# Second attention of a two-block transformer kernel: each pair's weight unit in one piece, second transpose behind the next scores, five other operations moved forward

## The reference, cut to what matters

```python
def _latent_token_mixer(h, kv_ctx, w_in, ...):
    k_a_c, v_a_c, k_b_c, v_b_c = kv_ctx
    proj = h @ w_in + b_in
    ...
    o_a = _windowed_attention(q_a, k_a, v_a, k_a_c, v_a_c, sink)
    o_b = _global_attention(q_b, concat([k_b, k_b_c]), concat([v_b, v_b_c]))
    return _merge_branches(o_a, o_b, proj[..., OFF_GA:], w_branch_a, w_branch_b, w_out)
```

## Time and profile before

| | before |
|---|---|
| median of three runs | 934.7 us (934.2 to 935.8) |
| the profiled execution | 935.65 us |
| its span, first to last instruction | 934.0 us |
| PE busy | 909.8 us, 97% |
| PE weight loads busy | 734.0 us, 79% |
| DVE busy | 720.4 us, 77% |
| ACT busy | 534.3 us, 57% |
| POOL busy | 161.6 us, 17% |
| mean granted TensorE clock | 0.995 |

### The profile page before, as it was taken

The page is one execution under the profiler, slowest core; times in us unless marked ns, Lnnn a source line. Parts: engine busy times, 40 slices in busy tenths (PEclk is TensorE's granted clock), DMA queues, the critical chain, the costliest instruction groups (busy, mean ns, idle before and its releaser), DMA issues.

```text
span 934.0 us, 13750 instructions
## 1 busy us (share of the span) xinstructions
PE 909.8 (97%) x4672; PEld 734.0 (79%) x4672; DVE 720.4 (77%) x1030; ACT 534.3 (57%) x830; POOL 161.6 (17%) x247
## 2 busy tenths in 40 slices
PE   8999999999999989999999999999999999999996
PEld 7888887777877878888888887666678788888885
DVE  4779476878778778887588788875668889999976
ACT  6775654475765556555433344756674676666643
POOL 7001000216600000110021001460000024444400
PEclk9999999999999999999999999999999999999998
DMA  9747744876552446887498856332235565555572
GB/s 317 201 149 221 252 139 140 265 267 195 171 179 84 135 152 220 266 271 256 162 351 295 274 167 202 97 89 88 87 112 175 168 193 174 174 174 176 171 261 72
DMA packets 100534, 176.16 MB, mean 189 GB/s; under 512 B 8560, under 2 KB 36592, under 8 KB 100352
## 3 DMA queue, kind: packets, MB, share of 16 engines
q1 hardware_dynamic: 93120, 149.87, 49.7%
q0 software_dynamic: 7184, 25.50, 8.1%
q10 hardware_dynamic: 176, 0.08, 0.0%
HBM read 174.38 MB, written 1.05 MB: 188 GB/s over the span
## 4 chain that ended last, share of the span: by engine, by line
PE 59%; DVE 4%; ACT 2%; issue 1%; DVEq 0%
PE acc L775 51%; PE turned L1245 2%; PE scores L1234 1%; PE turned L868 1%; PE turned L1347 1%; DVE wlo L1922 1%; PE turned L1134 1%; PE turned L1157 1%; PE turned L811 1%; ACT prob L1774 0%; DVE soft L2623 0%; DVE turn L2009 0%; ACT whi L1387 0%; PE turned L1249 0%; ACT turn L1831 0%
## 5 line engine op out<-in xcount | busy, mean ns | idle before, releaser
L1922 DVE TENSOR_TENSOR wlo<-raw,whi 128x1024 fp32r<-128x1024 f32 (+3 forms) x269 | 345.1, 1302 | 85.3 <-ACT whi L1387 74.6
L1387 ACT CAST whi<-raw 128x1024 fp32r<-128x1024 f32 (+3 forms) x269 | 273.4, 1034 | 163.7 <-PE acc L775 119.6
L775 PE MATMUL acc<-whi,lta_hi 128*128 128x512 f32 (+2 forms) x576 | 163.4, 399 | 0.2 <-DVEq L2498 0.2
L775 PE MATMUL acc<-whi,lta_lo 128*128 128x512 f32 (+2 forms) x576 | 155.8, 385 | 0.0
L775 PE MATMUL acc<-wlo,lta_hi 128*128 128x512 f32 (+2 forms) x576 | 155.3, 385 | 0.0
L775 PEld LDWEIGHTS acc<-whi,lta_hi 128*128 128x128 f32 x576 | 101.1, 188 | 31.8 <-issue 11.8
L775 PEld LDWEIGHTS acc<-whi,lta_lo 128*128 128x128 f32 x576 | 106.9, 188 | 22.4
L775 PEld LDWEIGHTS acc<-wlo,lta_hi 128*128 128x128 f32 x576 | 106.9, 188 | 21.9
L657 POOL DMA_DIRECT2D wm<-in_w_mod x48 | 34.5, 720 | 436.8 <-DVEq L2053 251.2
L775 PE MATMUL acc<-whi,ltb_hi 128*128 128x512 f32 (+1 forms) x268 | 73.8, 394 | 3.3 <-ACT whi L1387 2.4
L775 PE MATMUL acc<-whi,ltb_lo 128*128 128x512 f32 (+1 forms) x268 | 72.3, 388 | 0.2 <-DVE ltb_lo L2758 0.2
(11 more groups left out here) (370 smaller groups left out, 1307.1 us busy)
## 6 DMA issues: line engine op xcount, KB each, us to landing
raw<-in_w_in SPq DMA_DIRECT2D x88, 512.0 KB, 3.9
wm<-in_w_mod POOLq DMA_DIRECT2D x48, 512.0 KB, 5.5
raw<-in_w_up SPq DMA_DIRECT2D x88, 256.0 KB, 3.0
raw<-in_w_up SPq DMA_DIRECT2D x32, 512.0 KB, 4.5
raw<-in_w_down SPq DMA_DIRECT2D x32, 512.0 KB, 5.1
raw<-in_w_down SPq DMA_DIRECT2D x44, 256.0 KB, 3.2
raw<-in_w_o SPq DMA_DIRECT2D x8, 512.0 KB, 4.6
raw<-in_w_out SPq DMA_DIRECT2D x8, 512.0 KB, 3.8
```

The costliest lines, as they stand in the source:

```text
L775: ins = pe.matmul(acc[s][:, t, 0:n], lhs[part][:, kt0 + kk, tok], w[:, u % RING, kk, 0:n], start=(opens and k == 0 and kk == 0 and j == 0) ...
L1387: act.copy(whi[:, s, :, 0:n], raw[:, s, :, 0:n]).then_inc(hi_ready, 1)
L1922: dve.tensor_tensor(wlo[:, s, :, 0:n], raw[:, s, :, 0:n], whi[:, s, :, 0:n].bitcast(F32), ALU.subtract)\
```

## The change

In `attend_pairs` the second `PT` tile of a pair is transposed behind the scores of the next pair; this holds for MLA and AB. In AB the whole unit runs ahead of the values, and `ab_rest` keeps only the transposition. Four of the 24 first transposes go. ACT does one small activation on the identity ahead of its first wait for data. The copy of V0 moves behind those of `mqT` and `mkT`. `gate_on("G21")` moves ahead of a split. Around CX, ACT casts units between the groups of `hc` and goes through units ahead of the squares; DVE makes two groups of `hc` before each addition to x, and splits a unit between.

```diff
                 for p in range(n):
-                    for e in range(2):
-                        ... (wait, four transposes of prob[:, e], signal)
+                    turned_out(p, 0)
                     if p + 1 < n:
                         score(p + 1)
+                    turned_out(p, 1)
                     fill_units(p + 1)
                     ...
-            for _ in range(24):
+            for _ in range(20):
                 pe.transpose(sc[0][:, 0:P], ident[:], ident[:])
...
             def ab_rest(p):
                 if p > 0:
                     ab_turn(p - 1, 0)
-                ab_fill(p, (1,))
-            attend_pairs("AB", AB_PAIRS, ab_scores, 4, ab_values, lambda p: ab_fill(p, (0,)), ...)
+            attend_pairs("AB", AB_PAIRS, ab_scores, 4, ab_values, lambda p: ab_fill(p, range(T)), ...)
...ACT
+            act.wait_ge(ev("ident_ready"), 1)
+            act.activation(stat[:, 0, 8:9], ident[:, 0:1], ACT.Copy, scale=ident[:, 1:2])
             act.wait_ge(ev("columns_landed"), 16)
...
-            evac("V0", gv[:, :, 0:COLS])
+            ahead(last_unit("V0") + 1)
             for name, dst in (("mqT", mqT), ("mkT", mkT)):
                 t_out(name, dst.rearrange("p a b -> p (a b)"))
+            evac("V0", gv[:, :, 0:COLS])
...
-            lt_act("hc", ltb)
+            lt_act("hc", ltb, (0, 1))
+            ahead(PLAN.unit["WOB1"])
+            lt_act("hc", ltb, (2,))
+            ahead(PLAN.unit["WOB1"] + 1)
+            lt_act("hc", ltb, (3,))
+            ahead(PLAN.unit["CX"])
             act.activation(stat[:, 0, 8:9], one_col[:], ACT.Sqrt)
...
                 if c == 0:
-                    ahead(PLAN.unit["CX"])
+                    ahead(PLAN.unit["CX"] + 1)
...DVE
-            ahead(PLAN.unit["UKV0"] + 1)
             gate_on("G21", o_mem)
...
-            lt_dve("hc", ltb, modx[:, 8:16], modx[:, 0:8], sent=ctxT)
             for c in range(2):
+                lt_dve("hc", ltb, modx[:, 8:16], modx[:, 0:8], (2 * c, 2 * c + 1), sent=ctxT)
                 ... (addition to x)
+                if c == 0:
+                    ahead(PLAN.unit["WOB1"])
             ahead(PLAN.unit["CX"])
```

More of the change, by code:

```diff
@@ L860, in attend_pairs, with turned_out @@
                     fill_rest(0)
-                for p in range(n):
-                    for e in range(2):
[L863 to L869, removed]
+                def turned_out(p, e):
+                    i = 2 * p + e
+                    b, k = S_USE[f"{name}.{i}"]
+                    pe.wait_ge(s_free[b], k + 2)
+                    bank, full = t_begin(f"{name}.PT{i}")
+                    for j in range(blocks):
+                        ins = pe.transpose(bank[:, P * j:P * j + P], prob[:, e, P * j:P * j + P], ident[:])
+                    ins.then_inc(full, 1)
+                for p in range(n):
+                    turned_out(p, 0)
                     if p + 1 < n:
                         score(p + 1)
+                    turned_out(p, 1)
                     fill_units(p + 1)
@@ L1291, in ab_rest @@
                     ab_turn(p - 1, 0)
-                ab_fill(p, (1,))
-            attend_pairs("AB", AB_PAIRS, ab_scores, 4, ab_values, lambda p: ab_fill(p, (0,)), after=lambda p: ab_turn(p, 1),
+            attend_pairs("AB", AB_PAIRS, ab_scores, 4, ab_values, lambda p: ab_fill(p, range(T)), after=lambda p: ab_turn(p, 1),
                          fill_rest=ab_rest)
```

## The result

The kernel after takes 940.07 us (median of 5 runs, 939.91 to 940.60) against 934.7 us (5 runs, 934.1 to 935.8) of the kernel before: ratio 1.0058, 95% interval 1.0043 to 1.0072, so 0.6% slower. The forecast was 938.6 us, slower. Its profiled execution has a span of 938.5 us; before it was 934.0.

A forecast was written before the change was run, and what follows sets the result against it. PE, busy 909.8 of 934.0 us, was taken as the bound. 935.65 - 0.8 - 1.3 - 1.25 - 2.0 + 6.6 = 936.9 us, plus one clock fall of 1.7, gave 938.6; range 931 to 942.5.

The forecast's parts named there:

- The main step: AB: without the half unit behind the values PE waits for ACT and DVE, +1.2 us at each of seven places.
- R1: Rival: in AB the transposition is no obstacle, cover is not lost; total 927.1, or 932 with half lost; chance 0.13.
- R2: Rival: only AB's five transpositions cost, chains of pairs 0 and 2 fit, no clock fall; 934.1 us; chance 0.22.
- The chain behind pair 0: AB: DVE's norm sums and ACT's two table changes lose the half unit as cover, about +1.2 us.
- a switch: AB: one more change of matmul kind between scores and second tile, 0 to 0.1 us, taken as 0.05 a pair.
- The chain behind pair 2: AB: DVE's copy of IN3, ahead of pair 4's last exponential, loses the half unit as cover, about +1.2 us.
- The work saved: AB: a whole unit takes 2.85 us against 3.10 for two halves; less a switch, -0.2 us a pair.
- one fall of 1.7: Clock drops to half speed once behind new PE waits at the scaled x or in AB, +1.7 us.
- R3: Rival: the clock falls at most new waits, four falls of 1.7 us in AB and at CX; 943.7; chance 0.15.
- The small edits: Start, mqT and mkT, G21, MLA and CX: 0, -0.8, -1.3, -1.25 and -2.0 us.
- the new wait at the scaled x: CX: PE's 2.4 us wait goes, but PE stands 1.9 us at the transposes of the scaled x instead.
- The start: First matmul sooner by ACT's early table load, but transfers set the pace: 0, at best -0.3 us.

The follow-up runs named there:

- e1: Kernel after with AB's unit split again, first half behind the scores' second tile, second half behind the values: 930.02 us.
- e4: Kernel after with ACT's copy of a tile transposed behind the values moved behind the next pair's exponentials, PE's order unchanged: 931.10 us.
- e9: Kernel after with AB's unit in halves only behind the five pairs with a transposition (4, 5, 6, 9, 10): 932.02 us.
- e3: Kernel before with only the second transposed tile moved behind the next scores, in MLA and AB, AB's unit still in halves: 934.54 us.
- e7: e1 with the start as before: no early activation on ACT, 24 transposes: 929.83 us.
- e5: e1 with ACT's copy of a turned tile moved behind the next pair's exponentials: 927.15 us.
- e6: e5 with the unit whole ahead of the values behind pairs 7, 8 and 11 to 15, halves elsewhere: 927.32 us.
- e8: e1 with the CX edit undone on ACT and DVE: hc in one piece, table load and squares ahead of the cast of CX's first unit: 932.42 us.
- e2: Kernel before with only AB's unit in one piece between scores and values, both turned tiles still ahead of the scores: 951.31 us.
- e11: e5 with DVE's inverse of the norm sums behind the maxima of pair 2 instead of ahead of them: 927.52 us.

## Why the prediction was right

**The main step held.** That the loss sits where the half unit covered ACT and DVE was right in mechanism, in place (seven places) and in size: 1.25 a transposition against 1.2 forecast, 1.37 a chain against 1.2. e1 takes the whole loss back, e4 takes back most of it with PE's order untouched, e9 parts the transpositions from the chains. R1 (927 to 932) and R2 (934) are excluded by these. The signs came as well: with the clock up, periods of 8.78, 8.43 and 8.39 where 8.7 was forecast, the first `PT` at 2.19 behind pair 4's transposition and 2.01 behind the later ones. PE's waits there read 1.54 and 0.29, or 1.36 alone, where I said 1.8 and 0.4: the profile counts them from the end of the transposition (0.66 us long), and I had given it 0.4. The undisturbed pairs take 6.23 to 6.25 and not 6.1 to 6.2.

**The chain behind pair 0 was right in part by luck.** I gave it 1.2 for the lost half unit, and its period (from pair 2) rose by 1.37. But e1 and e3 keep the half unit, and there it is 8.02, already 0.79 above the 7.23 before. So the late tile made 0.79 of it and the whole unit only 8.60 - 8.02 = 0.58. In my sum the late tile was a switch and no more. ACT copies both transposed tiles ahead of its two table loads, and now the second comes later. PE's rows of e3, then ACT's of e3, then ACT's of the kernel before:

```profile
588.45 1.13 PE L1237 MATMUL scores<-kT_a,qT_a 64*128 64x512 f32 x4
...
595.20 0.66 PE L867 MATMUL turned<-ident,prob 128*128 128x128 f32 x4 [0.79 <-ACT prob L1777]
596.47 1.13 PE L1237 MATMUL scores<-kT_a,qT_a 64*128 64x512 f32 x4 [0.61 <-ACT prob L1777]
```

```profile
590.20 0.60 ACT L1447 ACTIVATE probT<-turned 128x512 f32<-128x512 f32 x1 [0.99 <-PE turned L867]
590.82 1.28 ACT L1441 ACT_TABLE_LOAD   x1
```

```profile
592.20 1.28 ACT L1438 ACT_TABLE_LOAD   x1
```

The first load starts 590.82 - 588.45 = 2.37 us behind the scores of pair 2 in e3, and 592.20 - 591.36 = 0.84 in the kernel before. That this delay is all of the 0.79 is read from these rows; no experiment moves it alone. The chain behind pair 2 is as forecast: its period (from pair 4) is 6.42 in e1 and 7.74 in the kernel after.

**The work saved was too high.** I took 0.25 for the unit and -0.05 for a switch, 0.2 a pair. Measured are 0.12, and the parts were wrong as well: e3 shows the late tile at -0.04, so the merged unit gives 0.1, and the whole unit took 2.94 in its place and not the 2.85 of the earlier trace rows, taken from a stretch with other neighbours. The other nine pairs gave 0.5 in all and not 1.8: 1.3 in eight periods, 0.44 of it from the late tile in the first, less the 0.8 behind the last scores. Together with the size of the places AB cost 8.4 us without falls, against 6.6.

**The clock.** I took one fall of 1.7; two came in the profiled execution, 1.6 and 1.5 us. Both followed waits in the pairs with transpositions, as forecast for "six or seven places"; the like waits at the other places were followed by none. R3 with four is too many for the profile and for the runs, which lie within 0.7 us of each other.

**The small edits** were forecast at -5.35. At ck -0.6 (-0.8), at UKV1 -1.5 (-1.3), in MLA -1.4 (-1.25) held. At CX the new wait at the scaled x came where forecast, but at 1.44 us and not 1.9, in PE's timeline of the kernel after:

```profile
340.43 1.09 PE L811 MATMUL turned<-ident,work 128*128 128x128 f32 x8 [1.44 <-DVE work L2543]
```

So like for like the edit gives 1.0 and not 0.3, and no fall came there. The start was forecast at 0, and e7 confirms it, though the profile alone seemed to say -0.96. The profiled execution comes to 935.65 - 0.96 - 0.6 - 1.5 - 1.4 - 2.6 + 8.4 + 3.1 = 940.1: gains of 1.7 more than forecast, 1.0 of it chance, stand against losses of 3.2 more. That the total came within 1.5 us owes something to these two misses having opposite signs.

**The rule that I set against the trace.** In TensorE: Matmul & The Clock Gate, Part 4 on the PE-mode transpose, the Trainium skill says that transposes don't count as busy for the clock. e1 shows the contrary directly, for these float32 transposes. Of its 20 first transposes the early ones start 0.21 to 0.22 us apart and the last 0.11, and nothing else had run on PE; the kernel after, where the clock rose later, needs longer for the same 20. PE's first rows in e1 and in the kernel after:

```profile
1.72 4.13 PE L916 MATMUL scores<-ident 128*128 128x128 f32 x20 [1.72 <-POOL ident L613]
```

```profile
1.72 4.53 PE L916 MATMUL scores<-ident 128*128 128x128 f32 x20 [1.72 <-POOL ident L613]
```

## What to carry to other kernels

Work of the bottleneck engine between two steps of a chain is cover: before moving it for a cheaper order, count what the other engines do in that gap, and find who waits for whom at each place. Here 0.1 us a pair was bought with 1.3 to 1.4 at six of sixteen pairs and 0.6 at a seventh (periods of the kernel after against those of e1, without the falls). The cheaper fix was on the engine that held the chain: an instruction whose input comes late belongs behind those whose input is there (e5, 927.15 us: 2.9 us below the repair of PE's order alone, and 1.0% below the kernel before). And an offset early in one profile is no gain until a kernel with that edit undone shows it.

## What the hardware showed unexpectedly

**The rise of the clock at the start has no fixed time.** Kernels with the same start show the granted clock at its upper level from 5.3 us (e1), 6.0 (e4, e5), 10.9 (after) or 11.0 us (e6) on, and medians don't follow it: e5 and e6 differ by 0.2 us. At 7 to 10 us the kernel after ran its first units at half speed and was within 0.3 us of e1 again by 28 us (28.00 against 27.73 for the transposes of the scaled x), where the transfers set the pace.

**A wait doesn't always bring a fall.** Behind the same 2.42 us at CX the clock fell in the profiles of before and of e8, and not in e3. Behind pair 2 it fell in e4, and not in the kernel after, whose waits there are the same. The falls cost 1.5 to 1.6 us each, and e2, with waits at most pairs, spread over 947.6 to 953.2 us, with a mean granted clock of 0.994 in the fastest run and 0.988 in the slowest.

**VectorE and GpSimd held each other up.** The 128x2 addition L2644 took 0.34 us in e5 and 1.25 in e11, where it began 0.05 us behind a GpSimd operation of 1.27 us and ended with it (592.44 + 1.25 = 593.69, 592.39 + 1.27 = 593.66). In SBUF — State Buffer, section SBUF: two separate sides, the Trainium skill says that a VectorE instruction with two SBUF inputs and a GpSimd instruction that reads SBUF take a shared port pair as an exclusive lock; these rows agree. The other way round, in e5 a GpSimd operation of 1.04 us (L700, at 589.32) took 2.05 us at 593.83, where it began 0.08 us behind VectorE's split of 1.23 us.
